# A two-part transformer kernel on one core: output projection by token tile inside the expert stage, and the linear recurrence in quarters

## What is computed

```
m = x @ w_in                                   # q, k, v, xr, gr, two gates
ya = differential attention(q, k, v)
c  = causal convolution of xr (4 taps)
r, i = sigmoid(block products of c + bias)     # 8 blocks of 128
a = exp(-8 r softplus(-lambda));  u = sqrt(1 - a^2) * (i * c)
s_t = a_t s_{t-1} + u_t;  yr = s * gelu(gr)    # the linear recurrence
merged = g0 * (ya @ w_br_attn) + g1 * (yr @ w_br_lru)
x = layer_norm(ALPHA x + merged @ w_out)       # the output projection
for each of 8 heads: 16 experts of 16384 per token, by product keys
    y += sum_j softmax_j * gelu(x . u[e_j]) * v[e_j]
x = layer_norm(ALPHA x + y)
```

## Time and profile before

| | us |
|---|---|
| median of 3 runs | 3753.79 (3752.42 to 3757.61) |
| profiled execution, its own time | 3749.74 |
| its span | 3747.9 |
| PE busy, share of the span | 3306.0 (88%) |
| DVE busy | 1661.0 (44%) |
| ACT busy | 700.3 (19%) |
| POOL busy | 597.8 (16%) |
| granted PE clock, mean | 0.939 of full |
| first gather of layer 1, of layer 2 | 2027.14, 3071.34 |

### The profile page before, as it was taken

The page is one execution under the profiler, slowest core; times in us unless marked ns, Lnnn a source line. Parts: engine busy times, 40 slices in busy tenths (PEclk is TensorE's granted clock), DMA queues, the critical chain, the costliest instruction groups (busy, mean ns, idle before and its releaser), DMA issues. The chain is left out here.

```text
span 3747.9 us, 46312 instructions
## 1 busy us (share of the span) xinstructions
PE 3306.0 (88%) x16666; PEld 2335.2 (62%) x16666; DVE 1661.0 (44%) x4108; ACT 700.3 (19%) x1536; POOL 597.8 (16%) x516
## 2 busy tenths in 40 slices
PE   8999679999989989999986888887899768888887
PEld 7886558888867978877865433443478654333433
DVE  2113542111154532111244877777412438677775
ACT  1100221101021211101231222222202312222222
POOL 0000000000000000000001545444200014444442
PEclk9999769999999989999987989999999889999998
DMA  4343013444422004443325999999733249999998
GB/s 175 146 160 112 1 45 115 156 148 145 148 98 90 4 21 146 153 152 137 136 101 199 409 422 422 422 422 422 319 147 139 86 173 406 422 422 422 422 421 347
DMA packets 113613, 827.82 MB, mean 221 GB/s; under 512 B 12528, under 2 KB 14064, under 8 KB 15120
## 3 DMA queue, kind: packets, MB, share of 16 engines
q0 software_dynamic: 73728, 536.90, 34.5%
q1 hardware_dynamic: 37184, 273.59, 19.7%
q10 hardware_dynamic: 2576, 15.59, 1.3%
HBM read 824.99 MB, written 1.05 MB: 220 GB/s over the span
## 5 line engine op out<-in xcount | busy, mean ns | idle before, releaser
L2507 PE MATMUL psum_all<-expert_rows,const_sb 128*128 128x512 f32 x2048 | 967.7, 630 | 199.4 <-ACT const_sb L2445 197.9
L2206 POOL DMA_INDIRECT expert_rows<-in_peer_uv_dram,head_experts x512 | 597.6, 1167 | 3105.9 <-issue 2127.8
L2507 PEld LDWEIGHTS psum_all<-expert_rows,const_sb 128*128 128x128 f32 x2048 | 402.7, 201 | 746.8 <-issue 474.2
L278 PE MATMUL psum_all<-xn,weight_ring 128*128 128x272 f32 (+1 forms) x3200 | 730.0, 391 | 9.5 <-DMA weight_ring<-in_ffn_in_dram 9.5
L2325 DVE CUSTOM_DVE_ANT_0 expert_rows<-expert_rows,xn 128x1024 f32<-128x1024 f32 x512 | 616.5, 1223 | 263.1 <-DMA expert_rows<-in_peer_uv_dram,head_experts 258.2
L278 PEld LDWEIGHTS psum_all<-xn,weight_ring 128*128 128x128 f32 x3200 | 611.3, 191 | 127.1 <-DMA weight_ring<-in_ffn_in_dram 9.5
L278 PE MATMUL psum_all<-hidden,weight_ring 128*128 128x272 f32 (+1 forms) x1408 | 318.6, 389 | 0.0
L278 PEld LDWEIGHTS psum_all<-hidden,weight_ring 128*128 128x128 f32 x1408 | 267.5, 190 | 50.5
L1879 PE MATMUL psum_all<-x,weight_ring 128*128 128x256 f32 x1024 | 227.7, 380 | 0.0
L2445 ACT ACTIVATE const_sb<-cst,head_weights 128x128 f32<-128x128 f32 x496 | 158.6, 390 | 312.4 <-DVE head_weights L2334 297.6
L1879 PEld LDWEIGHTS psum_all<-x,weight_ring 128*128 128x128 f32 x1024 | 192.0, 190 | 28.2 <-issue 2.7
(11 more groups left out here) (485 smaller groups left out, 3002.4 us busy)
## 6 DMA issues: line engine op xcount, KB each, us to landing
weight_ring<-in_ffn_in_dram SPq DMA_DIRECT2D x88, 1024.0 KB, 4.9
weight_ring<-in_w_in_dram SPq DMA_DIRECT2D x48, 1024.0 KB, 7.0
weight_ring<-in_ffn_out_dram SPq DMA_DIRECT2D x32, 1408.0 KB
weight_ring<-in_peer_q_dram SPq DMA_DIRECT2D x16, 1024.0 KB
weight_ring<-in_hyb_in_dram SPq DMA_DIRECT2D x12, 1024.0 KB, 4.9
wv<-in_w_v_dram ACTq DMA_DIRECT2D x8, 1024.0 KB, 5.7
weight_ring<-in_br_attn_dram SPq DMA_DIRECT2D x8, 1024.0 KB, 5.8
weight_ring<-in_br_lru_dram SPq DMA_DIRECT2D x8, 1024.0 KB
```

The lines of the kernel that those rows point to most:

```text
L278: mm = pe.matmul(banks[s * halves + h], wt[:, h, k, :], rhs[:, k, :], start=(k == 0), stop=(k == ktiles - 1))
L2206: pool.indirect_dma_start(out=rows[:, j, :], out_offset=None, in_=a["peer_uv"], in_offset=bass.IndirectOffsetOnAxis(ap=idx[:, n, j:j + 1], ...
L2507: mm = pe.matmul(sums(n, half), diag[:, j, :], rows[:, j, D + half * 512:D + (half + 1) * 512], start=False, stop=last and j == TOPK - 1)
```

## The change

The separate output projection stage is removed. Its products are done in the expert stage, eight output tiles for tokens 0 to 127 and then eight for tokens 128 to 255, each 128 columns wide, so the matrix is loaded twice. Sums, centring, scaling, squares and roots are done per token tile. The order on PE, DVE, ACT and SP is written out anew up to the second unit; the loop starts a head later. All sixteen products must be done before the first fourteen row slots are released, because the merged input now lies in the memory of `expert_rows`, as do the tiles of the stages before (`area`). The matrices of heads 0 and 1 are loaded in the branch stage into row slots 14 and 15; key matrix, query and search tiles move to the ring's other region. The search of tile 1 for head 0 and of tile 0 for head 1 is spread over the four batches of the first unit.

In the recurrence stage, gate products go tile by tile (both gates of a tile) between branch tiles, gelu comes first on ACT, and everything behind the exponentials is done in four quarters of two tiles (`QUARTERS`).

```diff
@@ storage and statistics tiles @@
-        ln_sum, ln_square, ln_next = xt[:, 1, 0:T2], xt[:, 1, T2:2 * T2], xt[:, 1, 2 * T2:4 * T2].rearrange("p (n t) -> p n t", n=2)
-        ln_temp = xt[:, 0, 0:T2]
+        ln_sum, ln_square, ln_next = xt[:, 0, 0:P], xt[:, 0, P:2 * P], xt[:, 0, 2 * P:4 * P].rearrange("p (n t) -> p n t", n=2)
+        ln_temp = (xt[:, 0, 4 * P:5 * P], xt[:, 1, 0:P])
+        late_squares = xt[:, 1, :].rearrange("p (k t) -> p k t", k=KD)
+        heads_in = ctx.enter_context(nc.semaphore("heads_in"))
+        arena = ctx.enter_context(nc.sbuf_tensor("expert_rows", [P, TOPK * 2 * D], F32))
+        rows = arena[:, :].rearrange("p (j d) -> p j d", j=TOPK)
...
@@ recurrence stage, DVE @@
-            dve.wait_ge(S.i_ready, 1)
-            dve.tensor_tensor(ig, ig, xc[:, :, :], ALU.mult)
-            dve.wait_ge(S.decays, 1)
-            step(dve.tensor_tensor(mult[:, :, :], decay[:, :, :], decay[:, :, :], ALU.mult))
-            dve.scalar_tensor_tensor(out=mult[:, :, :], in0=mult[:, :, :], scalar=1.0, in1=th, op0=ALU.add, op1=ALU.mult).then_inc(S.mult_ready, 1)
-            dve.wait_ge(S.roots, 1)
-            step(dve.memset(mult[:, :, 0:1], 1.0))
-            step(dve.tensor_tensor(mult[:, :, :], mult[:, :, :], ig, ALU.mult))
-            for k in range(KD):
-                last = dve.tensor_tensor_scan(xc[:, k, :], decay[:, k, :], mult[:, k, :], 0.0, ALU.mult, ALU.add)
-            step(last)
-            gate_branch(range(4, KD))
-            dve.wait_ge(S.gelu, 1)
-            step(dve.tensor_tensor(gr, gr, xc[:, :, :], ALU.mult))
+            for n, part in enumerate(QUARTERS):
+                dve.wait_ge(S.gate_in, 4 * (n + 1))
+                step(dve.tensor_tensor(ig[:, part, :], ig[:, part, :], xc[:, part, :], ALU.mult))
+            for n, part in enumerate(QUARTERS):
+                dve.wait_ge(S.decays, n + 1)
+                step(dve.tensor_tensor(mult[:, part, :], decay[:, part, :], decay[:, part, :], ALU.mult))
+                dve.scalar_tensor_tensor(out=mult[:, part, :], in0=mult[:, part, :], scalar=1.0, in1=th[:, part, :],
+                                         op0=ALU.add, op1=ALU.mult).then_inc(S.mult_ready, 1)
+            dve.wait_ge(S.gelu, 1)
+            for n, part in enumerate(QUARTERS):
+                dve.wait_ge(S.roots, n + 1)
+                step(dve.memset(mult[:, part, 0:1], 1.0))
+                step(dve.tensor_tensor(mult[:, part, :], mult[:, part, :], ig[:, part, :], ALU.mult))
+                for k in range(2 * n, 2 * n + 2):
+                    last = dve.tensor_tensor_scan(xc[:, k, :], decay[:, k, :], mult[:, k, :], 0.0, ALU.mult, ALU.add)
+                step(last)
+                step(dve.tensor_tensor(gr[:, part, :], gr[:, part, :], xc[:, part, :], ALU.mult))
+            gate_branch(range(4, KD))
@@ recurrence stage, PE @@
-            branch(range(0, 4))
+            branch(range(0, 2))
             pe.wait_ge(S.gate_weights, 16)
...
+            gate(range(0, 3))
+            branch(range(2, 3))
+            gate(range(3, 6))
+            branch(range(3, 4))
+            gate(range(6, KD))
             branch(range(4, KD))
@@ recurrence stage, ACT: gelu first, signals per quarter @@
+            act.activation(gr, gr, ACT.Gelu_apprx_tanh).then_inc(S.gelu, 1)
             act.activation(gates, gates, ACT.Sigmoid).then_inc(S.branch_gates, 1)
...
-            act.activation(mult[:, :, :], mult[:, :, :], ACT.Sqrt).then_inc(S.roots, 1)
-            act.activation(gr, gr, ACT.Gelu_apprx_tanh).then_inc(S.gelu, 1)
+            for n, part in enumerate(QUARTERS):
+                act.wait_ge(S.mult_ready, n + 1)
+                act.activation(mult[:, part, :], mult[:, part, :], ACT.Sqrt).then_inc(S.roots, 1)
@@ branch stage, SP @@
                         w.first(sp, 0, tile["w_out2"], W2)
+                        for hd in range(2):
+                            sp.dma_start(rows[:, TOPK - 2 + hd, :], tile["peer_q"](hd)).then_inc(heads_in, 16)
@@ the output projection's own block (L2103 to L2144) is removed @@
...
@@ expert stage, SP @@
-                        sp.dma_start(keys[:, :, :], a["sub_keys"][l]).then_inc(S.keys_in, 16)
-                        w.rest(sp, 1, tile["peer_q"], W2, PH, S.query_ready, 1)
+                        for i in range(2, KD):
+                            sp.wait_ge(S.w_ready, 2 * i - 2)
+                            sp.dma_start(w.slot(0, i % 2, W2), tile["w_out2"](i % (KD // 2))).then_inc(w.landed[0][i % 2], 16)
+                            if i == 3:
+                                sp.dma_start(keys[:, :, :], a["sub_keys"][l]).then_inc(S.keys_in, 16)
+                        sp.wait_ge(S.w_ready, 2 * KD)
+                        for sem in w.landed[0]:
+                            sp.sem_clear(sem)
+                        for hd in range(2, PH):
+                            if hd >= 4:
+                                sp.wait_ge(S.query_ready, hd - 1)
+                            sp.dma_start(w.slot(0, hd % 2, W2), tile["peer_q"](hd)).then_inc((S.even_head, S.odd_head)[hd % 2], 16)
@@ expert stage, DVE @@
+                        def add_out(t):
+                            m, tok = t % KD, slice(t // KD * P, (t // KD + 1) * P)
+                            dve.wait_ge(S.w_ready, t + 1)
+                            dve.scalar_tensor_tensor(out=h[:, m, tok], in0=h[:, m, tok], scalar=ALPHA, in1=psum[t % 4][:, 0:P], op0=ALU.mult, op1=ALU.add).then_inc(S.w_read, 1)
...
-                        for n in range(QT):
-                            normalise(n)
-                            for piece in (find_first_keys,) + pieces[1:]:
-                                piece(0, n)
-                            shift(n)
+                        first_tile_sums()
+                        add_out(KD)
+                        centre(0)
+                        add_out(KD + 1)
+                        scale(0)
+                        add_out(KD + 2)
+                        find_first_keys(0, 0)
+                        add_out(KD + 3)
+                        for piece in pieces[1:]:
+                            piece(0, 0)
+                        shift(0)
+                        for t in range(KD + 4, 2 * KD):
+                            add_out(t)
+                        centre(1)
+                        scale(1)
+                        dve.wait_ge(S.x_in, 1)
...
+                        unit(0, 0, (second_tile_starts, second_tile_found, next_head_starts, next_head_found))
                         dve.wait_ge(S.x_in, QT)
-                        with step.loop(PH - 2, QT * 21) as i:
+                        unit(0, 1, True)
+                        with step.loop(PH - 3, QT * 21) as i:
@@ expert stage, PE @@
-                        pe.sem_inc(S.slot_free, TOPK)
...
+                        def out_product(t):
+                            pair, tok = t // 2, slice(t // KD * P, (t // KD + 1) * P)
+                            if t % 2 == 0:
+                                pe.wait_ge(w.landed[0][pair % 2], 16 * (pair // 2 + 1))
+                            if t >= 4:
+                                pe.wait_ge(S.w_read, t - 3)
...
+                        for t in range(KD + 1):
+                            out_product(t)
+                        pe.wait_ge(S.summed, KD - 1)
+                        pe.matmul(mean, ones, ln_sum, start=True, stop=True)
+                        pe.wait_ge(S.square_summed, KD - 1)
+                        pe.matmul(mean_square, ones, ln_square, start=True, stop=True).then_inc(S.ln_sums, 1)
+                        out_product(KD + 1)
+                        out_product(KD + 2)
+                        pe.wait_ge(heads_in, 16 * 2)
+                        first_query(0)
+                        pe.wait_ge(S.keys_in, 16)
+                        first_scores(0)
+                        out_product(KD + 3)
+                        turn_in(0)
+                        for t in range(KD + 4, 2 * KD):
+                            out_product(t)
+                        pe.wait_ge(S.w_ready, 2 * KD)
+                        pe.sem_inc(S.slot_free, TOPK - 2)
+                        pe.wait_ge(S.x_in, 1)
...
+                        first_query(1)
+                        first_scores(1)
+                        pe.sem_inc(S.slot_free, 1)
+                        turn_in(1)
...
                         find_scores(1)
+                        pe.sem_inc(S.slot_free, 1)
```

236 lines of the change are left out of this document (135 added, 101 removed).

## The result

Forecast: 3714 us, range 3704 to 3738. Measured in the same rounds: **3706.8 us** after (four runs, 3703.9 to 3709.5) against 3753.1 before (four runs, 3750.0 to 3757.6). The ratio is 0.9881 with the 95% interval [0.9869, 0.9893]: 44.7 us less by the ratio, 46.3 by the medians.

A forecast was written before the change was run, and what follows sets the result against it. Transfers bound the expert phases: sixteen full queues at 422 GB/s, 651 us per layer. Gains of 26 (projection), 7 (quarters) and 6.4 (dry queues), 39.4 us, off the median 3753.79 gave 3714 us, range 3704 to 3738.

The forecast's parts named there:

- Part 1: Recurrence stage in quarters: roots come 4.7 us earlier, tail grows from 10.8 to about 12.0; 3.5 us per layer, 7 in all.
- Part 2: Output projection by token tile: first gather at S+42.4 instead of S+56.6, S being its first product; 13 us per layer, 26 in all.
- The upper bound of 15.5: Output projection: largest gain per layer, 15.5 us, if the second token tile's first product does not wait.
- Part 3: Start of the gather stream: seventeenth gather arrives in time, so the queues no longer run dry; 6.4 us for both layers.
- the dry stretch: Gather queues behind the late seventeenth gather: 344 and 321 GB/s for 15 us, 2.8 and 3.6 us lost.
- Pacing: Rival, projection: products at 0.131 us and loads 1 us slower, start only 9 us earlier per layer; 3727 us, chance 0.14.
- Stall: Rival, expert stage: one more remote wait of 12.6 us per layer delays the refill; 3735 us, 0.10; doubled 3754, 0.02.
- Clock: Rival, projection on PE: waits for loads keep it at 1.2 GHz, 0.222 us per instruction; 17 us slower, 3771, chance 0.04.
- No effect: Rival, gather stream: its end is not tied to its start, only the quarters and little else count; 3747 to 3757, chance 0.03.

The follow-up runs named there:

- the kernel with the resident weights: Changed kernel with the second token tile's products starting at the weight tiles still in the ring, four loads instead of six: 3707.3 us, ratio 0.9886 to the kernel before.
- the longer delay: Changed kernel plus seven reciprocals per layer on VectorE in the search for the second unit's experts, behind the first gathers: 3727.0 us, ratio 0.9934 to the kernel before.
- the kernel with the early gate products: Changed kernel with the gate products of tiles 3 to 7 all ahead of the fourth branch tile: 3701.4 us, ratio 0.9872 to the kernel before.
- the kernel with the old recurrence stage: Changed kernel with the recurrence stage put back as it was, projection by token tile kept: 3715.5 us, ratio 0.9908 to the kernel before.
- the two experiments on the recurrence stage: Recurrence stage put back in the changed kernel, 3715.5 us; recurrence stage of the change alone in the kernel before, 3744.3 us.

## Why the prediction was right, step by step

**Part 1, mis-sized.** Predicted 3.5 us per layer, found 2.8 once the first 32 products are taken out (2.2 and 1.8 with them). The step that failed: "four times (0.1 + 0.6 + 2x0.6 scan + 0.6 + hand-offs)" for 12.0 us of tail. A 512-column operation takes 0.69 us with the next one 0.73 behind it, where a quarter of 2.29 is 0.57, so the tail is 12.9, and the next stage starts 1.9 us later behind the roots, not 1.2. The 4.7 us by which the roots come earlier was right (29.0 against 24.3); against the first product only 3.9 showed, since the first products took 0.8 longer. "Interleaving gives nothing, because a branch tile stands ahead of the last four products" fits the sigmoids' end (R+24.3; the tanh began at R+23.6 before), and the runs turn it round: moving that tile behind them gave 3.5 us per layer, more than the quarters' 2.8.

**Part 2, right, in part by luck.** Predicted 13 per layer, found 13.8 and 12.8. Inside: mean S+21.0 (predicted 21.0), scores S+30.3 (29.8), first gather S+42.8 (42.4), last product S+40.6 (39.6). Two errors cancel ahead of the mean. The sum let the projection start at the low clock, for 1.7 us; its first 64 products ran at 1.00 in both layers (7.38 us; before, the granted clock of its first 5 us was 0.66 in the first layer and 1.00 in the second), and the load for product 8 was asked for at S+12.4 instead of 13.7. But it took 6.1 us and not 4.8 (below), so product 8 started at S+18.4, near the predicted 18.6. The slots are free 2.2 us ahead of the first gather, not 3. The upper bound of 15.5, product 8 not waiting, was reached and passed by the kernel with the resident weights: 16.4 and 15.7 earlier than before.

**Part 3, right in size, in part by luck.** Seventeenth gather +38.0 and +37.7 (predicted +35 to +45), the dry stretch gone, and with it 2.7 and 3.6 us (predicted 2.8 and 3.6). But the stream is 7.6 shorter and not 6.4 for reasons that the sum did not have: 4.9 us gained in the first ten us of the gathers and 3.7 given back at the end. The prediction took it that loads ran beside the first gathers "again"; before, the queues held nothing else then (SP's next load was asked for at 2039.19, 12 us behind the first gather). That the start of the stream moves its end "one for one", as the expectation had it and the sum assumed, is wrong in general: 3 of 5.4 us. It did no harm here, since from S to G the change shortened what stands ahead of both the gathers and these loads, and since the loads now fill the queues while the gathers start.

In sum the three parts gave 26.6+5.6+7.6 = 39.8 us against the 39.4 forecast: 1.4 too much in part 1, 0.6 and 1.2 too little in the others. That these errors cancel so nearly is luck; the rest of the 40.9 lies in code that the change doesn't touch.

**The rivals.** *Pacing*: in part. Product 8 waited 2.49 us for a load asked for at 1979.09 and used at 1985.15, 6.1 us with the key matrix ahead of it, against the 4.8 of a load alone; the products themselves ran at 7.38/64 = 0.115 us. *Stall*: ACT had one remote wait of 9.1 us and 8.8 in the other layer, and the refill was in time all the same. Its price was too low: it gave 7 us of dry queues to a refill at +51.6, and the longer delay, at +51.3 and +51.5, cost 10.6 and 9.0. *Clock*: fell. The projection waits for loads 3.9 us in all and is at 1.00 in all its windows. The Trainium skill, page "TensorE: Matmul & The Clock Gate", section "HAM oscillation — how this bites in real kernels", tells that the low clock comes back again and again with narrow tiles whose products (about 2 us) are shorter than the wait for the next load (about 3 to 5 us). Here the waits were 0.3 to 2.5 us behind runs of 1.9 to 7.4 us. The prediction's "by it the result would be this rival's" carried the page over to a case that it does not describe, and no run here has waits as long as the page's to try it. *No effect*: fell.

## What to carry to other kernels

Where one resource runs full for hundreds of microseconds, ask what is ahead of the moment from which it stays full, and count the bytes that can pass in the gap: a start that came 5.4 us later cost 3, because 4.5 us of other transfers were then out of the way while the gathers alone lost 2.7. Before splitting an elementwise chain for overlap, look at the order of the engine that feeds it: moving one tile of unrelated products behind the last gate product gave more than the quarters. When an effect of under 10 us is looked for in a kernel of 3700, cut the traces at fixed events and compare stretch by stretch, and put the cut behind instructions whose time varies from execution to execution: that turned 2.2 and 1.8 us into 2.8 and 2.8. The times alone could not tell apart two kernels whose way to the first gather differed by 5.6 us.

## What was not expected of the hardware

The same instructions, in code that no kernel here edits, take one of two times. Sixteen products of eight rows and 256 columns ahead of the second layer's recurrence stage, in the profile after and then in the kernel with the early gate products:

```profile
2902.76 7.19 PE L259 MATMUL psum_all<-rs,cst 8*128 8x256 f32 x16 [2.31 <-DVE rs L1965]
```

```profile
2899.81 4.32 PE L259 MATMUL psum_all<-rs,cst 8*128 8x256 f32 x16 [2.31 <-DVE rs L1965]
```

and the last block of sixteen weighted sums ahead of the turn of the first token tile, in the profile after and in the kernel with the old recurrence stage:

```profile
2648.18 7.13 PE L2600 MATMUL psum_all<-expert_rows,const_sb 128*128 128x512 f32 x16 [2.81 <-ACT const_sb L2512]
```

```profile
2652.72 8.83 PE L2587 MATMUL psum_all<-expert_rows,const_sb 128*128 128x512 f32 x16 [2.81 <-ACT const_sb L2499]
```

The windows that hold the small products, the profile after first:

```profile
2896.00:2911.00 15.00, 11.65 (x30) 6.49 (x28) 5.58 (x9) 0.80 (x3) 0.00 (x0) 0.61 0.00 0
```

```profile
2893.00:2905.00 12.00, 8.82 (x30) 4.52 (x28) 5.34 (x9) 0.81 (x2) 0.00 (x0) 0.78 0.00 0
```

Before them TensorE was busy without a break at 1.00; then it pauses twice, 2.5 and 2.3 us. Whether the clock falls to its lower level of 1.2 GHz for them differs from execution to execution: the sixteen take 4.3 to 4.7 or 6.7 to 7.2 us, and over the thirteen traces the stretch from the next layer's first product to R is 231.2 to 232.7 or 234.1 to 235.0. The last block takes 7.13 or 8.83 us, and in layer 1 the stretch from the last dot product to the next layer goes with it: 10.3 to 11.3 or 11.9 to 12.0. This is what the two experiments on the recurrence stage showed outside it, as far as it is explained: 1.6 of the 8.3 in one, 2.9 and 0.7 of the 7.6 in the other; it accounts for 1.7 less and 0.9 more in the table above as well. At the start of the recurrence stage it is the first 32 products, as told above. What decides between the values wasn't tried; each is a throw of 1 to 3 us on the path, and several of them together are as large as the effects looked for here. Another 3.3 us that the kernel with the stage undone had more (1.2 from S to G, 1.1 from G to D, 1.0 behind the last dot product) stay open.
